# Feed-forward gate and up tiles as seven block products of 256 tokens (Strassen), in three parts

## What is computed

```python
D_FF = 2816                                   # 22 tiles of 128
def _swiglu(x, w_gate, w_up, w_down):
    return (jax.nn.silu(x @ w_gate) * (x @ w_up)) @ w_down
x = x + MACARON * _swiglu(_rmsnorm(x, ffn1_norm), ffn1_w_gate, ffn1_w_up, ffn1_w_down)   # first block: 4 of them
...
def swiglu(h, w_gate_up, w_down):
    g, u = jnp.split(h @ w_gate_up, 2, axis=-1)
    return (jax.nn.silu(g) * u) @ w_down
x = x + swiglu(rms_norm(x, ffn_norm[layer]), ffn_w_gate_up[layer], ffn_w_down[layer])    # second block: 2
```

## Time and profile before

| | |
|---|---|
| median of three runs (lowest, highest) | 3212.49 us (3212.03, 3212.80) |
| span of the profiled execution | 3210.8 us |
| median less this span | 1.7 us |
| PE busy | 3203.0 us of the span |
| DVE, ACT, POOL busy | 1548.0, 1086.8, 1327.6 us |

### The profile page before, as it was taken

The page is one execution under the profiler, slowest core; times in us unless marked ns, Lnnn a source line. Parts: engine busy times, 40 slices in busy tenths (PEclk is TensorE's granted clock), DMA queues, the critical chain, the costliest instruction groups (busy, mean ns, idle before and its releaser), DMA issues.

```text
span 3210.8 us, 36140 instructions
## 1 busy us (share of the span) xinstructions
PE 3203.0 (100%) x14706; PEld 2655.4 (83%) x14706; DVE 1548.0 (48%) x1849; ACT 1086.8 (34%) x1449; POOL 1327.6 (41%) x550
## 2 busy tenths in 40 slices
PE   9999999999999999999999999999999999999999
PEld 7888888888888888888888877888888888888888
DVE  6442266554234431476444268545444486454421
ACT  4222333322232223333222355543223475432222
POOL 4444433544444444434444433235444212254443
PEclk9999999999999999999999999999999999999999
DMA  4223322322232322322323332323323333232222
GB/s 153 98 98 100 120 82 79 108 97 97 98 108 97 99 99 99 123 79 87 104 92 100 108 93 73 124 92 105 99 92 102 99 98 126 99 106 98 98 92 86
DMA packets 93236, 321.54 MB, mean 100 GB/s; under 512 B 10512, under 2 KB 14992, under 8 KB 93072
## 3 DMA queue, kind: packets, MB, share of 16 engines
q1 hardware_dynamic: 87680, 312.07, 29.4%
q10 hardware_dynamic: 5392, 7.17, 0.7%
HBM read 316.05 MB, written 2.10 MB: 99 GB/s over the span
## 4 chain that ended last, share of the span: by engine, by line
PE 99%; DVE 0%; ACT 0%; DMA 0%; issue 0%; ACTq 0%; DVEq 0%
PE bank L383 20%; PE bank L387 20%; PE bank L384 20%; PE bank L398 9%; PE bank L399 9%; PE bank L405 9%; PE bank L368 1%; PE bank L369 1%; PE bank L372 1%; PE bank L696 0%; PE bank L824 0%; PE bank L823 0%; PE bank L565 0%; PE bank L829 0%; PE bank L558 0%; PE bank L559 0%
## 5 line engine op out<-in xcount | busy, mean ns | idle before, releaser
L2600 POOL TENSOR_TENSOR wlo<-raw,whi 128x1024 fp32r<-128x1024 f32 x535 | 1324.3, 2485 | 1862.9 <-ACT whi L1017 1862.5
L1017 ACT ACTIVATE whi<-raw 128x1024 fp32r<-128x1024 f32 x588 | 611.3, 1052 | 585.3 <-PE bank L405 413.2
L383 PE MATMUL bank<-gxh,whi 128*128 128x512 f32 x1536 | 600.4, 391 | 0.0
L384 PE MATMUL bank<-gxl,whi 128*128 128x512 f32 x1536 | 597.7, 389 | 0.0
L398 PE MATMUL bank<-gxh,whi 128*128 128x512 f32 x1248 | 487.3, 390 | 1.3 <-ACT whi L1017 1.2
L399 PE MATMUL bank<-gxl,whi 128*128 128x512 f32 x1248 | 485.7, 389 | 0.0
L383 PE MATMUL bank<-f_hh,whi 128*128 128x512 f32 x1034 | 402.2, 389 | 0.0
L384 PE MATMUL bank<-f_hl,whi 128*128 128x512 f32 x1034 | 402.2, 389 | 0.0
L387 PE MATMUL bank<-gxh,wlo 128*128 128x512 f32 x1536 | 379.6, 389 | 0.0
L1832 DVE TENSOR_TENSOR f_u<-bank,R 128x512 f32<-128x512 f32 x132 | 91.2, 691 | 582.9 <-PE bank L405 582.9
L383 PEld LDWEIGHTS bank<-gxh,whi 128*128 128x128 f32 x1536 | 288.4, 188 | 60.9 <-issue 0.7
(11 more groups left out here) (415 smaller groups left out, 3584.7 us busy)
## 6 DMA issues: line engine op xcount, KB each, us to landing
raw<-stream SPq DMA_DIRECT2D x588, 512.0 KB, 3.3
xa_mem<-memT ACTq DMA_DIRECT2D x2, 1024.0 KB, 6.2
m_dk<-decay ACTq DMA_DIRECT2D x2, 514.0 KB, 4.5
x<-xT ACTq DMA_DIRECT2D x4, 256.0 KB, 5.3
x<-xT SPq DMA_DIRECT2D x4, 256.0 KB, 6.7
outT<-x SPq DMA_DIRECT2D x2, 512.0 KB, 3.0
m_ct<-cos ACTq DMA_DIRECT2D x2, 256.0 KB, 2.7
m_sn<-sin ACTq DMA_DIRECT2D x2, 256.0 KB, 3.1
```

Source lines behind the costliest of these rows:

```text
L383: pe.matmul(out, seq(hi, k, P), h, start=first and k == 0, stop=False)
L384: pe.matmul(out, seq(hi, k, P), l, start=False, stop=False)
L1017: act.activation(M.whi[r][:, :], M.raw[r][:, :], ACT.Copy).then_inc(*S.tick("hi", u))
L2600: pool.tensor_tensor(M.wlo[r][:, :], M.raw[r][:, :], M.whi[r][:, :].bitcast(F32), ALU.subtract).then_inc(*S.tick("lo", u))
```

## The change

In each feed-forward stage, tiles 0 and 1 stay as they are (`PLAIN = 2`). For tiles 2 to 21 the gate and up units together are read as a 2 by 2 block matrix (gate or up by first or second half of the 1024 inputs), the activations as another (half of the inputs by half of the tokens), and the 2 by 2 product is made of seven block products instead of eight, each 4 input chunks deep and 256 tokens wide: 12 matmuls. So a tile is 84 matmuls of 256 tokens instead of 48 of 512. This needs new things:

- **Sums of weights**, per tile: DVE makes `s13` (1024 columns) and two more sums s2, s4 (512 each, into banks 5 and 6), ACT rounds them (`s13_hi` into the gate's `whi` slot, `s24_hi` into `sh`, and `m22_hi`), DVE makes their rests (`s13_lo`, `s24_lo`); POOL makes the rest of `m22` (512 columns) and of the up unit.
- **Sums of activations**, once a stage (`turned`: `th`, `tl`): four chunks k, each with four DVE sums of 256 columns (`turn_parts`) out of `gained` (ACT, `take_gain`), two ACT copies (`turn_hi`) and two DVE rests (`turn_lo`). Chunks 0 and 1 are begun in the stage before (at its output tiles 5 to 7) in stages f = 1 to 5; chunks 2 and 3, and all four for f = 0, stand after `rstd` and ahead of tile 0's `gate`.
- **Sums of products**: the seven go into one pair of banks in the order 1, 5, 6, 2, 7, 3, 4. ACT saves three intermediate results (`snap1`, `snap5`, `snap6`), and DVE adds them back (`c22`, `first_row`). PE waits for `snap1` and `snap5` and `snap6` ahead of products 6, 2 and 7, for `c22` ahead of product 4. No product of the next tile stands between.

Beside this the hidden tiles are used in three parts (0 to 5, 6 to 13, 14 to 21) through a ring of nine: after tile 6 and tile 14 PE does eight output units of the part that is ready, and DVE adds each to `x`. The output products now see a DVE multiplication by `R` first (`scaled_part`), as `R` is no longer in the up result. The copy that made `f_hh` moves from DVE to ACT. The order of POOL's work swaps gate and up.

```diff
+F_PARTS = ((0, 6), (6, 14), (14, 22))
+F_RUNS = ((0, 7), (7, 15), (15, 22))
+PLAIN = 2
...
@@ tensor_program, ffn
+        def product(n, m, weights, lo_event, moving, out, first, arrive=None):
+            hi, lo = weights
+            for k in range(4):
...
+                pe.matmul(out, seq(hi, k, P), moving[k][0], start=first and k == 0, stop=False, skip_group_check=n != 1)
+                pe.matmul(out, seq(hi, k, P), moving[k][1], start=False, stop=False, skip_group_check=n != 1)
+            pe.wait_ge(*S.at(*lo_event))
+            for k in range(4):
+                mm = pe.matmul(out, seq(lo, k, P), moving[k][0], start=False, stop=k == 3, skip_group_check=n != 1)
+            mm.then_inc(*S.tick("seven", f, m, n))
...
+        def quad(m):
...
+            product(1, m, (seq(M.whi[u], 0), seq(M.wlo[u], 0)), up_lo, gx_part[1, 1], x[:, 0:HALF], True)
...
+            pe.wait_ge(*S.at("s13_hi", f, m))
+            product(5, m, (seq(M.whi[g], 0), seq(M.wlo[g], 0)), ("s13_lo", f, m), turns[0], y[:, HALF:], True,
+                    [("turned_lo", f, k) for k in range(4)] if m == PLAIN else None)
+            pe.wait_ge(*S.at("s24_hi", f, m))
+            pe.wait_ge(*S.at("snap1", f, m))
+            product(6, m, (seq(sh, 1), seq(sl, 1)), ("s24_lo", f, m), turns[2], x[:, 0:HALF], False)
+            pe.wait_ge(*S.at("snap5", f, m))
+            product(2, m, (seq(M.whi[u], 1), seq(M.wlo[u], 1)), up_lo, gx_part[2, 1], y[:, 0:HALF], False)
+            pe.wait_ge(*S.at("snap6", f, m))
+            product(7, m, (seq(M.whi[g], 1), seq(M.wlo[g], 1)), ("s13_lo", f, m), turns[1], x[:, 0:HALF], False)
+            product(3, m, (seq(sh, 2), seq(sl, 2)), ("s24_lo", f, m), gx_part[2, 2], y[:, HALF:], False)
+            fourth(m)
...
@@ scalar_program, ffn
+        def run(c):
+            first, end = max(F_RUNS[c][0], PLAIN), F_RUNS[c][1]
+            for m in range(first, end):
+                x, y, more = bank[BANK["a", f, m]], bank[BANK["u", f, m]], m + 1 < end
+                split_hi(U["up", f, m + 1] if more else U["down", f, c, 0])
+                snap(1, m, x[:, 0:HALF], T["c16"][:, 0:HALF], "c1")
+                if more:
+                    s13_hi(m + 1)
...
+                snap(5, m, y[:, HALF:], T["c5"][:, :], "c22")
+                if more:
+                    s24_hi(m + 1)
+                if m > first or c == 0:
+                    silu(m - 1)
+                snap(6, m, x[:, 0:HALF], T["c16"][:, HALF:], "c1")
+                if more:
+                    m22_hi(m + 1)
+                if m > first or c == 0:
+                    hidden_hi(m - 1)
...
@@ vector_program, residual and ffn
+            if i + 1 in F_STAGE:
+                f = F_STAGE.index(i + 1)
+                if m >= 6:
+                    turn_lo(f, m - 6)
+                if m in (5, 6):
+                    turn_parts(f, m - 5)
...
+        def run(c):
+            first, end = max(F_RUNS[c][0], PLAIN), F_RUNS[c][1]
+            for m in range(first, end):
+                before, more = m > first or c == 0, m + 1 < end
+                if more:
+                    sums(m + 1)
+                    s13_lo(m + 1)
+                if before:
+                    gate(m - 1)
+                if more:
+                    s24_lo(m + 1)
+                if before:
+                    gated(m - 1)
+                if before:
+                    hidden_lo(m - 1)
+                c22(m)
+                first_row(m)
...
+        rstd(i)
+        dve.wait_ge(*S.at("rstd", i))
+        for k in range(2 if f else 0, 4):
+            turn_parts(f, k)
+            turn_lo(f, k)
+        gate(0)
+        gated(0)
+        hidden_lo(0)
+        begin(PLAIN)
+        for c in range(2):
+            run(c)
+            for m in range(KD):
+                dve.wait_ge(*used("down", f, c, m))
+                scaled_part(f, c, m, at_bank("part", f, c, m)[:, :], M.R)
+                dve.scalar_tensor_tensor(seq(M.x, m), T["u"][:, :], F_SCALE[f], seq(M.x, m), ALU.mult, ALU.add).then_inc(
+                    *S.tick("part_sum", f, c, m))
+                if m == 4:
+                    begin(F_RUNS[c][1])
+        run(2)
+        residual(i, lambda m: ("down", f, 2, m), F_SCALE[f])
```

More of the change, by code:

```diff
@@ L127 @@
 SHARED = {
+    "f_vector": "s13 s13_lo s2 s4 s24_lo c1 c22 turned_parts turned_lo part_scaled part_sum kept_rstd",
+    "f_scalar": "s13_hi s24_hi snap1 snap5 snap6 gained turned_hi hh",
     "m1_vector": "ga ws rot_table gsum gsq centred diagonal col_rstd vsum vbias z0 ginv vn hinv ret_n ret_g y1h y1 rot_c rot_s rot_in rope gg sm "
@@ L1080, in ffn, with silu @@
         i, T = F_STAGE[f], M.f[f]
-        for m in range(KF):
-            ahead(("gate", f, m))
-            if m == 0 and not f:
-                root(i)
-            ahead(("up", f, m))
-            if m == 0 and f:
-                root(i)
+        def silu(m):
             act.wait_ge(*S.at("a", f, m))
@@ new lines, in begin @@
+        def begin(m):
+            split_hi(U["up", f, m])
+            s13_hi(m)
+            s24_hi(m)
+            m22_hi(m)
+        ahead(("gate", f, 0))
+        if not f:
+            root(i)
+        ahead(("up", f, 0))
+        if f:
+            root(i)
+        else:
+            take_gain(0, 0)
+            turn_hi(0, 0)
+            take_gain(0, 1)
+            turn_hi(0, 1)
+            take_gain(0, 2)
+        turn_hi(f, 2)
+        take_gain(f, 3)
+        turn_hi(f, 3)
+        silu(0)
@@ new lines, in ffn @@
+        hidden_hi(0)
+        begin(PLAIN)
+        for c in range(2):
+            run(c)
+            ahead(("down", f, c, 0))
+            ahead(("down", f, c, 1))
+            silu(F_RUNS[c][1] - 1)
+            hidden_hi(F_RUNS[c][1] - 1)
+            for m in range(2, KD - 2):
+                ahead(("down", f, c, m))
+            begin(F_RUNS[c][1])
+        run(2)
+        ahead(("down", f, 2, 0))
+        ahead(("down", f, 2, 1))
+        silu(KF - 1)
+        hidden_hi(KF - 1)
+        residual(i, [None, None] + [("down", f, 2, m) for m in range(2, KD)])
@@ new lines, in begin, with run @@
+        def begin(m):
+            sums(m)
+            s13_lo(m)
+            s24_lo(m)
+        def run(c):
+            first, end = max(F_RUNS[c][0], PLAIN), F_RUNS[c][1]
[14 more added lines that the diff above has]
+                first_row(m)
+            m = end - 1
+            gate(m)
+            gated(m)
+            hidden_lo(m)
```

339 lines of the change are left out of this document (263 added, 76 removed).

## The result

The changed kernel takes 3364.46 us (median of 4 runs, 3360.62 to 3364.7), before it was 3212.64 (4 runs, 3212.03 to 3213.14): 1.047 times as long, 95% interval 1.0455 to 1.0485. The prediction said 3301, between 3210 and 3350. The sign is right, the size is 64 us short.

The account below looks back on a forecast made before the run. PE bounds the kernel (99% of the chain). Steady tiles -47.0, last tiles -14.9, first tiles +17.4, heads +115.7, ends +15.2, program's end +2: +88.4 us, 3210.8 to 3299.2, with 1.7 between span and median 3300.9; range 3210 to 3350.

Parts of the forecast that it names:

- The tile: Steady tile with seven products: 10.32 us instead of 10.88, product 7 startable at 6.0 instead of 5.74; 84 tiles, -47.0 us.
- the handoff: Time for PE to start after another engine's result: taken as 0.17 us, bounds 0.05 to 0.25.
- the chain: In each steady tile, product 7 waits for snapshot 6, behind silu, `f_a`, `s13_lo`, `s13_hi` and snapshot 1; tile 10.32, not 10.05.
- The short split of POOL: POOL's 512-column split, taken as 1.25 us; rival (0.10): it costs as much as the long one, tile 11.3, total 3385.
- The first sum: DVE's `s13` in a tile, 1024 columns, priced at 1.22 us; in steady tiles its delay by POOL's split stays hidden.
- The start of a run: Tiles 7 and 15, after eight output units: late `s13` makes products 2 and 7 wait; 1.45 us, 12 times, +17.4.
- the 0.83 of the pace: Saving per tile if 84 short matmuls run at PE's pace: 10.05 us against 10.88, 100 us at best over 120 tiles.
- The head: First tiles of each stage: turning and sums delay tile 2; 16.9 us lost in four, 25.2 at f = 2, 22.9 at f = 0.
- The ends: Last eight outputs of a stage: DVE's backlog delays the last `gxl`; 7.6 us lost after f = 3 and f = 4 each.
- "nothing" for the mixers: Mixers after f = 0 and f = 2 need the last input only at 16 us: no loss.
- The clock: Rival (0.10): clock falls to 1.2 GHz in some 14 long waits at the heads, 1 to 2 us each: 3315 to 3330.

Follow-up runs that it names:

- The run of the three parts alone: The changed kernel with every tile computed as before the change, without the seven products, turning or sums; three parts and R on outputs kept: 3276.7 us, 1.02.
- fillers: Small multiplications of the ones tile into an unused bank, issued by PE ahead of its long waits in the changed kernel: 3442.4 us; with half as many, 3340.0 us.

## Why the prediction was right in sign and wrong in size

**The tile.** Predicted 10.32, measured 10.24, with one gap, before product 7, as the prediction put it. It is 0.16 us and not 0.27: in the tile that starts at 658.86, snapshot 6 ends 5.76 after the start, not 5.85, the pace up to product 7 takes 5.76, not 5.74, and the handoff 0.16, near my 0.17. The swap of snapshot 6 and silu showed the chain.

**The short split of POOL**, taken as 1.25, costs 1.30 (median of 120; 1.28 at least); that rival is out. The first sum was taken at 1.22; it has a median of 2.1, because POOL's split stops it, and nothing waited in steady tiles (min, median, max in ns):

```profile
L2091 DVE TENSOR_TENSOR f_s<-raws x120: 1210/2126/3420, 46.6 to 3284.5; 128x1024 f32<-128x1024 f32 x120
```

**The start of a run**: 2.28 us of waits in the sum (1.45, and the 0.83 of the pace), 2.58 (tiles 7) and 2.06 (tiles 15) measured, 27.8 in all against 27.4. Right, and shown by moving the sums.

**The head.** For f = 1 step by step from the last output's end at 595.6: x at 5.1 (5.1), `gxl` done at 7.8 (7.85), the wait 4.97 apart (4.9), the first `f_a` ends at 29.3 (28), product 1 at 32.5 (31), product 7 at 47.1 (45.7), tile 2 ends at 53.0 (50.0). The last 1.6 of these 3.0 are half clock behind the wait before product 7. The order that I laid end to end is the kernel's:

```profile
600.67 0.68 DVE L2019 SCALAR_TENSOR_TENSOR x<-bank,x 128x512 f32<-128x512 f32 x1
602.66 0.75 DVE L2028 SCALAR_TENSOR_TENSOR gxl<-x,lcol,gxh 128x512 fp32r<-128x512 f32 x1 [1.31 <-ACT gxh L1171]
...
612.17 3.35 DVE L1860 RECIPROCAL R<-sd 128x512 f32<-128x512 f32 x1 [1.13 <-ACT sd L1123]
...
624.20 0.68 DVE L2131 SCALAR_TENSOR_TENSOR f_a<-bank,R 128x512 f32<-128x512 f32 x1
```

In waits, the heads have 107.3 us against 120.7 in the sum (the 115.7, and the 0.8 by which tile 2 would be shorter), but 32 us of the slow matmuls are in them too.

**The ends, a term mis-sized.** I had 15.2 us after f = 3 and 4 and "nothing" for the mixers. Measured are 32.5 more than before and 8. The cadence at those outputs is 6.06 at the end of f = 3, not 5.5, since DVE adds a second sum there (L2042, 0.6 us an output), and the next mixer's angles (6.4 us of DVE, from 1913.96) stand ahead of the second output. ACT makes an output's `whi` behind the squares of the output three before it, and these wait for `x`. So PE waits 7.3 us for the fifth output's `whi` at the end of f = 3, and 5.2 for the seventh's at the end of f = 4 (where 6.9 us of DVE for that mixer's rates stand ahead of the fourth output). My chain did not look at this:

```profile
1921.08 0.69 DVE L2016 SCALAR_TENSOR_TENSOR x<-f_u,x 128x512 f32<-128x512 f32 x1
```
```profile
1923.57 1.04 ACT L1115 ACTIVATE whi<-raws 128x1024 fp32r<-128x1024 f32 x1
```
```profile
1924.75 0.76 PE L424 MATMUL bank<-f_hh,whi 128*128 128x512 f32 x1 [7.27 <-ACT whi L1115]
```

The waits for the mixers' last two `gxl` come to 15.1 us, by the names of my term just its 15.2; that is luck, since PE arrives there 5 to 7 us later than I had it and DVE's cadence is longer. After f = 0 and 2 the last input is not waited for, as I had it; the same backlog holds the last output's bank, 3.6 us too long each time, and I had looked at the inputs alone. The run of the three parts alone shows all three waits without a single product.

**The clock, the step that failed.** "If it went to 1.2 GHz in each of some 14 long waits" stood among the rivals at 0.10, outside the sum. It did go, in 30 places, not 14, because waits of 2.2 to 2.7 us count too and a head has up to three; and it costs 55.4/30 = 1.8 us in each, the upper part of my 1 to 2 (1.4 to 1.5 behind the waits at the starts of runs, up to 3.3 in a head). The mechanism is shown twice: fillers take it away, and a wait put in the kernel before brings it. How much of the 55 us the changed kernel would give back with the same waits stays between 25 and 55, and over 32 if the misplaced fillers are counted off. The rest of the miss: ends and mixers +25.3, heads -13.4, steady tiles -8.9 (84 x 0.164 instead of 0.27), pace +4.5, the rest +1; with the 55.4 that is the 64.

## What to carry to other kernels

Price a new wait of TensorE of 2 us or more at its length and 1.5 to 2 us on top, and put that in the sum, not among the rivals. A change that saves work on the engine in front moves its load to those behind: follow these through the places where the pipeline is empty (a stage's first tiles, a run's first tile, the last outputs), for there a tile's average says nothing. Ask there for everything that TensorE waits for: its input, its weights and its bank. And where a DVE operation with two SBUF inputs runs beside POOL's split, it took 1.9 to 2.8 us here instead of 0.69; with one input in PSUM it kept its 0.69.

## What was not expected of the hardware

After a wait TensorE's 512-column matmuls stand 0.427 us apart, the 256-column ones 0.213; at the full clock it is 0.2267 and 0.120. So the half clock makes them 1.88 and 1.78 times as long, not twice. The Trainium skill (TensorE: Matmul & The Clock Gate, Wait — 56ns, not 53.3ns?) gives columns/1.2 for the cold array, with which both rows agree, and columns/2.4 + 2.5 ns for the warm one, 0.216 for 512 columns and 0.109 for 256, where the matmuls here take 0.2267 and 0.120.

A wait of 2.2 us could bring the half clock, and one of 2.7 could be without it: tile 7 of f = 0 and of f = 3 and tile 15 of f = 0 have none behind the same wait that brings it in nine others, and no row tells why.
